# First tile's first 22 rows multiplied beside the product keys, 12 of them summed there

## The chip, the core and the metric

One core of a Trainium2 chip runs the whole program in one launch. The metric is device time in microseconds. The kernel before took 4780.42 us, the median of 3 runs (4776.94 to 4783.93).

## What is computed

The trunk has two layers on 256 context and 512 latent tokens of width 1024: a gated linear attention in layer 0 and a differential attention in layer 1, each followed by a PEER expert mixer (layer 0 on all 6 tiles of 128 tokens, layer 1 on the 4 latent tiles). The change touches the mixer only:

```python
def block(xc):                       # 128 tokens
    q = (xc @ wq).reshape(C, 8, 2, 128)
    s = einsum('chzd,zkd->chzk', q, subkeys)          # 128 keys a side
    top_s, top_i = lax.top_k(s, 16)
    cand_s = top_s[:, :, 0, :, None] + top_s[:, :, 1, None, :]
    best_s, best_j = lax.top_k(cand_s.reshape(...), 16)
    g = softmax(best_s)                               # 8 heads x 16 experts
    ue, ve = u[idx], v[idx]
    act = gelu(einsum('cd,chkd->chk', xc, ue))
    return einsum('chk,chkd->cd', g * act, ve)
```

So every token has 128 pairs (8 heads of 16), each with a row of U and a row of V, out of 16384.

## The kernel before

The stages of a layer follow each other with a meeting of all five engines between them (`run`). Three of them matter here.

**The keys** (`product_keys`) take 16 steps, one for each head and side: step j is side j % 2 of head j // 2. SyncE loads the weights of the step, ScalarE rounds them (L1548), GpSimd subtracts for the low part (L1571), TensorE projects with 24 matmuls for each segment (L1518), ScalarE takes the queries (L1554), TensorE scores them against the keys (L1526), and VectorE finds the strongest 16 of every tile in four rounds (L1590 to L1606). The steps run in a hardware loop, two by two, and projection runs a step ahead of the scores.

**The experts** (`peer`) treat the tiles in two ways. The last ones, three in layer 0 and two in layer 1, are *sparse*: each pair's rows of U and V are gathered from memory. The others are *dense*: all experts are multiplied and a table of gates picks. The choice of a tile (`choose`, L2059 to L2073) searches the best 16 of each head's candidates (`search`), decodes them into key numbers (`decode`) and makes the indices of the gathers and the softmax weights. The order is the first sparse tile, the dense ones, then the other sparse ones. The first sparse tile is decoded in two halves of four heads, so that its gathers can start after the first half.

A sparse row passes through a pipe. GpSimd gathers U into one of 4 slots and V into one of 8 (L1784, L1791), row by row in one order. VectorE multiplies U with the token (`products`, L2081), ScalarE applies gelu (L1899), VectorE multiplies with the weight (`shares`, L2088), and then, for the first tile's first 96 rows, ScalarE makes a diagonal matrix of it (L1913) and TensorE sums the V row with it into PSUM banks 2 and 3 (`spread`, L1801). The later rows are summed by VectorE (L2106). Rows go in groups of two. 6 groups are multiplied beside the second tile's choice, between its pieces; 42 go beside the *lots*.

A lot is 8 tokens of a dense tile: VectorE makes one-hot places (L2112), ScalarE gates them (L1905), TensorE multiplies (L1818), ScalarE takes the result (L1922), and every fourth lot SyncE writes 2 MB of gates to memory. 16 lots are a dense tile: three blocks in layer 0, two in layer 1, and a transposed choice (`turn`, L1808) stands before each block. In layer 0 every lot also has a product of the modulation's weights w_mod (L321) of 0.5 MB, with two buffers: the load (L312) of the next but one waits for the product. At the end of the blocks comes the **key loop** (L1827, L1836), 128 keys of dense scores and values, in which the rest of the rows are gathered and summed.

Of the kernel before, what the change touches and what calls it, by code (L numbers as in the profile page):

```python
# [9 lines left out]
F32 = mybir.dt.float32  # L10
# [41 lines left out]
ROWS_FIRST = (96, 96)  # L52
ROWS_END = KEYS - 2
# [395 lines left out]
def norm(B, layer, gain, shift, scale, segs, split=0, ahead=None):  # L449
# [3 lines left out]
    if split:  # L453
        ar.take(KEYS_AHEAD)
# [1009 lines left out]

def product_keys(B, layer, segs):

    t0, n_tok = segs[0][0], sum(seg[1] for seg in segs)
    tiles = n_tok // P
    top, top_key = best_of(B, tiles)
    top_key = top_key.bitcast(U32)  # L1470
    ar, parts = Arena(B.peer_arena), Arena(B.part_arena)
    w_raw = [ar.take(C * P) for _ in range(2)]
# [5 lines left out]
    found_i = ar.take(tiles * TOPK, U32).rearrange("p (n k) -> p n k", n=tiles)  # L1478
    w_in, w_before = [B.kept(f"keys_w_in{s}") for s in range(2)], 16 * HEADS * layer
    names = ("const_in", "iota_in", "w_high", "w_split", "q_mm", "q_ev", "s_mm", "s_ev", "chain", "passed")  # L1480
    const_in, iota_in, w_high, w_split, q_mm, q_ev, s_mm, s_ev, chain_s, passed = (
        B.kept("keys_const_in") if x == "const_in" else B.sem(x) for x in names)
    ps = B.ps
    ahead_tiles = [tiles - SPARSE_TILES[layer], 0][:SEARCHED[layer]]
    cand = [[ar.take(CAND) for _ in range(2)] for _ in ahead_tiles]
    won, won_j = ([ar.take(TOPK, dt) for _ in ahead_tiles] for dt in (None, U32))
    best, best_j = kept_best(B)
    counted, place = ar.take(P), [ar.take(TOPK, U32) for _ in range(2)]
    PASSES = ((0, 0), (0, 1), (1, 0))
    Q_BANK = (0, 6)  # L1490

    def settle(dve):

        dve.sem_inc(passed, 1)
# [9 lines left out]
    def sync(sp):  # L1504
        sp.dma_start(counted, B.a["iota"]).then_inc(iota_in, 16)
        for j in range(2, 2 * HEADS):
            sp.wait_ge(w_split, j + 1)
            load(sp, j, j % 2)

    def tensor(pe):  # L1510
        def project(j, z):

            pe.wait_ge(w_split, j + 3)
            pe.wait_ge(q_ev, j + 1)
            for (s0, m, which) in segs:
                todo = [(c, a, b) for c in range(C) for a, b in PASSES]
                for at, (c, a, b) in enumerate(todo):
                    mm = pe.matmul(ps[:, Q_BANK[z] + which, 0:m], w[z][:, a, c, :], B.xr[:, b, c, s0:s0 + m],  # L1518
                                   start=at == 0, stop=at == len(todo) - 1)
            mm.then_inc(q_mm, 1)  # L1520

        def score(j, z):
            pe.wait_ge(q_ev, j + 3)
            pe.wait_ge(s_ev, j + 1)
            for t in range(tiles):
                mm = pe.matmul(ps[:, 2 + 2 * z + t // 4, t % 4 * P:t % 4 * P + P],  # L1526
                               q[z][:, t * P:t * P + P], keys[:, z, :], start=True, stop=True)
            mm.then_inc(s_mm, 1)

        pe.sem_inc(q_mm, 2)  # L1530
        pe.wait_ge(const_in, 16 * layer + 16)
        project(0, 0)
        with pe.Fori(0, HEADS - 1) as i:
            project(2 * i + 1, 1)
            score(2 * i, 0)
            project(2 * i + 2, 0)
            score(2 * i + 1, 1)
        project(2 * HEADS - 1, 1)
        score(2 * HEADS - 2, 0)
        score(2 * HEADS - 1, 1)  # L1540

    def scalar(act):
        act.sem_inc(q_ev, 2)

        def split_w(j, z):
            act.wait_ge(w_in[z], 8 * j - 8 * z + 16 + w_before)
            act.wait_ge(q_mm, j + 1)
            act.copy(w[z][:, 0].rearrange("p c n -> p (c n)"), w_raw[z]).then_inc(w_high, 1)  # L1548

        def take(j, z):  # L1550
            act.wait_ge(s_ev, j + 1)
            act.wait_ge(q_mm, j + 3)
            for (s0, m, which) in segs:
                ins = act.copy(q[z][:, s0 - t0:s0 - t0 + m], ps[:, Q_BANK[z] + which, 0:m])  # L1554
            ins.then_inc(q_ev, 1)

        split_w(0, 0)
        split_w(1, 1)
        with act.Fori(0, HEADS - 1) as i:
            for z in range(2):  # L1560
# [696 lines left out]
```

## Time and profile before

| | layer 0 | layer 1 |
|---|---|---|
| keys, TensorE's first projection to VectorE's last | 954 to 1127 | 3434 to 3542 |
| first tile's choice | 1131 to 1159 | 3547 to 3576 |
| second tile's choice with 12 rows | 1159 to 1199 | 3576 to 3616 |
| lots | 1199 to 1566 (48) | 3616 to 3892 (32) |
| key loop | 1590 to 2760 | 3913 to 4730 |

The profiled execution took 4767.23 us, of which 4765.6 are the span from the first to the last instruction; its mean granted TensorE clock is 0.929. Times in the table are us from the span's start. Over the span TensorE is busy 87%, VectorE 70%, GpSimd 38% and ScalarE 27%. A busy share is an average over stages with different limits; the stage tables say which engine is near its bound in each.

### The profile page before, as it was taken

What the parts mean: (1) busy time and instruction counts of PE and PEld (TensorE: products, weight loads), DVE (VectorE), ACT (ScalarE), POOL (GpSimd) and SP (SyncE); (2) the same over time, 40 slices, a digit from 0 to 9 for tenths busy, and PEclk for the clock granted to TensorE, in tenths of its full rate; (3) what the DMA queues carried; (4) which work ended last, traced back from release to release, by engine and by line L of the source; (5) the groups of instructions that cost most, each with busy time, mean ns of one, the idle gap of its engine ahead of it and who ended that gap; (6) DMA issues with size and microseconds to landing.
All of it is one profiled execution on the core that took longest, in us unless ns stands there. A gap on an engine that the chain in (4) does not pass through costs nothing.

```text
span 4765.6 us, 53250 instructions
## 1 busy us (share of the span) xinstructions
PE 4164.2 (87%) x18407; PEld 2864.9 (60%) x18407; DVE 3321.5 (70%) x6651; ACT 1309.2 (27%) x2628; POOL 1799.4 (38%) x1652
## 2 busy tenths in 40 slices
PE   7999976694998899999999979886667879999997
PEld 3776664383776666666666645553353446666665
DVE  2466665568779677787777846676589767777776
ACT  3231311211666211111111123332114552222222
POOL 0012111022665555656566600000127755554452
PEclk8999978797998999999999989997788999999998
DMA  7966785713998999999999936888619999999995
GB/s 242 284 197 199 230 236 145 246 58 116 360 396 330 395 363 400 398 387 390 371 391 391 393 125 175 227 226 224 195 55 331 383 369 399 391 391 400 392 389 226
DMA packets 514577, 1408.03 MB, mean 295 GB/s; under 512 B 45692, under 2 KB 128892, under 8 KB 509470
## 3 DMA queue, kind: packets, MB, share of 16 engines
q1 hardware_dynamic: 330014, 733.73, 46.1%
q0 software_dynamic: 184320, 671.17, 36.4%
q8 instruction: 139, 2.28, 0.2%
q14 instruction: 104, 0.85, 0.1%
HBM read 1226.46 MB, written 178.26 MB: 295 GB/s over the span
## 4 chain that ended last, share of the span: by engine, by line
PE 62%; DVE 14%; DMA 12%; POOL 4%; ACT 4%; issue 3%; SPq 0%; DVEq 0%; ACTq 0%; POOLq 0%
PE ps L1836 19%; PE ps L1827 17%; DMA peer_arena<-in_peer_u 4%; PE ps L1518 3%; DMA u_rows<-mixer_arena 3%; PE ps L746 3%; PE ps L1801 2%; DMA expert_rows<-u_rows,peer_arena 2%; PE ps L1227 2%; PE ps L1232 2%; DVE expert_rows L2081 2%; PE ps L749 2%; PE ps L321 2%; PE ps L815 1%; POOL expert_rows L1791 1%
## 5 line engine op out<-in xcount | busy, mean ns | idle before, releaser
L1784 POOL DMA_INDIRECT expert_rows<-u_rows,peer_arena x640 | 836.8, 1308 | 1038.9 <-DVE expert_rows L2081 809.7
L1827 PE MATMUL ps<-part_arena,peer_part_arena 128*128 128x384 f32 (+1 forms) x4096 | 1028.4, 333 | 39.3 <-DVE peer_part_arena L2118 26.7
L2081 DVE SCALAR_TENSOR_TENSOR expert_rows<-expert_rows,mixer_in 128x1024 f32<-128x1024 f32 x640 | 764.2, 1221 | 140.8 <-DMA expert_rows<-u_rows,peer_arena 138.4
L1791 POOL DMA_INDIRECT expert_rows<-in_peer_v,peer_arena x640 | 760.8, 1189 | 207.0 <-issue 185.2
L1827 PEld LDWEIGHTS ps<-part_arena,peer_part_arena 128*128 128x128 f32 x4096 | 698.5, 189 | 113.9 <-issue 104.3
L1836 PE MATMUL ps<-best,peer_arena 128*128 128x512 f32 x1540 | 685.3, 592 | 0.0
L1827 PE MATMUL ps<-mixer_in_parts,peer_part_arena 128*128 128x384 f32 (+1 forms) x2048 | 633.0, 309 | 0.0
L2106 DVE SCALAR_TENSOR_TENSOR peer_arena<-expert_rows,peer_arena 128x1024 f32<-128x1024 f32 x445 | 571.7, 1285 | 34.7 <-DVE peer_arena L2106 1.4
L1801 PE MATMUL ps<-expert_rows,peer_arena 128*128 128x512 f32 x768 | 376.1, 638 | 163.6 <-ACT peer_arena L1913 163.3
L1836 PEld LDWEIGHTS ps<-best,peer_arena 128*128 128x128 f32 x1540 | 285.1, 189 | 296.0 <-issue 296.0
L1571 POOL TENSOR_TENSOR part_arena<-peer_arena,part_arena 128x1024 fp32r<-128x1024 f32 x32 | 76.5, 2392 | 1004.9 <-ACT part_arena L1548 1004.9
L2118 DVE TENSOR_TENSOR peer_part_arena<-peer_arena,peer_part_arena 128x1024 fp32r<-128x1024 f32 x256 | 312.9, 1222 | 154.0 <-ACT peer_part_arena L1929 153.6
L1827 PEld LDWEIGHTS ps<-mixer_in_parts,peer_part_arena 128*128 128x128 f32 x2048 | 386.6, 189 | 55.0 <-issue 55.0
L1899 ACT ACTIVATE peer_arena<-peer_arena 128x2 f32<-128x2 f32 x320 | 65.3, 204 | 1176.1 <-DVE expert_rows L2081 1176.0
L1801 PEld LDWEIGHTS ps<-expert_rows,peer_arena 128*128 128x128 f32 x768 | 150.7, 206 | 335.9 <-issue 214.4
L1058 POOL TENSOR_TENSOR mixer_arena<-mixer_arena 128x64 f32<-128x64 f32 x168 | 82.4, 490 | 645.1 <-ACT mixer_arena L902 645.1
L2172 DVE TENSOR_TENSOR peer_arena<-peer_arena 128x384 f32<-128x384 f32 (+1 forms) x256 | 124.8, 488 | 254.4 <-ACT peer_arena L1964 254.0
L1929 ACT CAST peer_part_arena<-peer_arena 128x1024 fp32r<-128x1024 f32 x256 | 266.0, 1039 | 110.8 <-DMA peer_arena<-in_peer_u 110.6
L1964 ACT ACTIVATE peer_arena<-ps 128x384 f32<-128x384 f32 (+1 forms) x256 | 110.8, 433 | 558.8 <-PE ps L1827 558.7
L367 DVE STREAM_TRANSPOSE mixer_arena<-mixer_arena 128x512 f32<-128x512 f32 x272 | 169.4, 681 | 117.1 <-DMA u_rows<-mixer_arena 93.9
L1518 PE MATMUL ps<-ffn_in_parts,part_arena 128*128 128x512 f32 (+1 forms) x1152 | 231.6, 360 | 11.7 <-POOL part_arena L1571 11.7
L1836 PE MATMUL ps<-peer_arena 128*128 128x512 f32 x520 | 231.5, 592 | 0.0
(273 smaller groups left out, 6050.9 us busy)
## 6 DMA issues: line engine op xcount, KB each, us to landing
peer_arena<-in_peer_u SPq DMA_DIRECT2D x256, 512.0 KB, 12.8
best<-in_peer_v SPq DMA_DIRECT2D x154, 512.0 KB, 9.0
mixer_arena<-in_peer_u SPq DMA_DIRECT2D x272, 256.0 KB, 7.4
u_rows<-mixer_arena SPq DMA_DIRECT2D x136, 512.0 KB, 4.7
hidden<-in_peer_u SPq DMA_DIRECT2D x240, 256.0 KB, 6.3
u_rows<-hidden SPq DMA_DIRECT2D x120, 512.0 KB, 5.1
gates<-peer_arena SPq DMA_DIRECT2D x20, 2048.0 KB, 10.6
peer_arena<-in_peer_v SPq DMA_DIRECT2D x52, 512.0 KB, 8.1
```

Of the source, the lines that this page charges most:

```text
L367: dve.transpose(self.outside[t][:, b % 2 * 512:b % 2 * 512 + 512], self.inside[s].rearrange("p (a c i) -> p c a i", a=4, i=P)[:, :, :, 32 ...
L746: pe.matmul(out, left, right, start=start, stop=stop)
L1518: mm = pe.matmul(ps[:, Q_BANK[z] + which, 0:m], w[z][:, a, c, :], B.xr[:, b, c, s0:s0 + m], start=at == 0, stop=at == len(todo) - 1)
L1784: pool.indirect_dma_start(u_ring[:, k % U_SLOTS, :], None, u_table, bass.IndirectOffsetOnAxis(u_index[s][:, m:m + 1], 0)).then_inc(u_row_i ...
L1791: pool.indirect_dma_start(v_ring[:, k % V_SLOTS, :], None, v_table, bass.IndirectOffsetOnAxis(v_index[s][:, m:m + 1], 0)).then_inc(v_row_i ...
L1801: mm = pe.matmul(ps[:, 2 + half, :], diag[m % V_SLOTS], v_ring[:, m % V_SLOTS, half * 512:half * 512 + 512], start=m == 0, stop=m == first ...
L1827: mm = pe.matmul(ps[:, 6, 0:dense_tok], left[j % len(left)][:, c, :], right[:, c, :], start=at == 0, stop=at == len(todo) - 1)
L1836: mm = pe.matmul(ps[:, 2 * n + half, :], wt[j % 2][:, n * P:n * P + P], v[j % BUFS][:, half * 512:half * 512 + 512], start=j == 0, stop=j ...
L1929: act.copy(u_high[j % 2], u[j % BUFS]).then_inc(u_rounded, 1)
L2081: dve.scalar_tensor_tensor(out=rows, in0=rows, scalar=1.0, in1=B.x[:, :, rows_at + s * P:rows_at + s * P + P], op0=ALU.mult, op1=ALU.mult, ...
L2106: dve.scalar_tensor_tensor(out=to, in0=rows, scalar=w, in1=to, op0=ALU.mult, op1=ALU.add).then_inc(y_ok, 1)
L2118: dve.tensor_tensor(u_low[j % BUFS], u[j % BUFS], u_high[j % 2].bitcast(F32), ALU.subtract).then_inc(u_split, 1)
```

## The change

Both layers get it. In `product_keys` the hardware loops are unrolled (the find of a step is now `strongest`), and:

- After step 3, when both sides of heads 0 and 1 are known, VectorE chooses these two heads of the first sparse tile (`choose` in the keys: `search_pairs`, `decode_pairs`, `index_pairs`, which are the old `search` and `decode` as functions).
- From step 5 on each step ends with a group of two products: 11 groups, 22 rows. Groups 0 to 7 get their shares two steps later; groups 0 to 5, 12 rows, are summed on TensorE in steps 10 to 15, behind the scores.
- GpSimd gathers U rows 0 to 25 and V rows 0 to 15 there, into 4 + 4 slots of their own, behind the subtraction of each step and after the last step.
- PSUM: banks 2 and 3 are the sum's from the start; of the scores the tiles from the fifth on, and of the queries the context segment, now share one bank for both sides, with a wait for the step before.
- The iota table, which the experts also loaded, is loaded only once, in the keys.

In `peer` the first choice has the other six heads, in one part. 8 groups (11 to 18) are multiplied beside the pieces of both choices; 29 groups in place of 42 are left for the lots. GpSimd goes on with V row 16; U rows follow from 26 on. The loads of w_mod wait for row 15's sum, since their buffers lie on the early slots. The key loop keeps its rows.

```diff
+EARLY_HEADS, CHOSEN_BEHIND, EARLY_FROM = 2, 3, 5
+EARLY_GROUPS, EARLY_GELUS, EARLY_SHARES, EARLY_SUMS = 11, 8, 8, 6
+U_EARLY, V_EARLY = 4, 4
+U_ROWS_EARLY, V_ROWS_EARLY = 26, 16
 # product_keys
     def tensor(pe):
         def project(j):
             z = j % 2
             pe.wait_ge(w_split, j + 1)
             if j >= 2:
                 pe.wait_ge(q_ev, j - 1)
             for (s0, m, which) in segs[::-1]:
                 if which == 0 and j:
                     pe.wait_ge(q_ev, j)
...
+                if t == 4 and j:
+                    pe.wait_ge(s_ev, j)
...
+        for j in range(STEPS):
+            if j + 1 < STEPS:
+                project(j + 1)
+            score(j)
+            if group_at(j) >= 5:            # group_at(j) = j - EARLY_FROM
+                spread(group_at(j) - 5)
     def scalar(act):
...
+        for j in range(STEPS):
+            take(j)
+            if j + 2 < STEPS:
+                split_w(j + 2)
+            if j == CHOSEN_BEHIND + 1:
+                exp()
+            if group_at(j) >= 3:
+                gelus(group_at(j) - 3)
+            if group_at(j) >= 5:
+                diagonals(group_at(j) - 5)
     def gpsimd(pool):
...
+        def gather_u(a):
+            if a == 0:
+                pool.wait_ge(index_ok, 1)
+            for k in range(GROUP * a, GROUP * a + GROUP):
+                if k >= U_EARLY:
+                    pool.wait_ge(score_ok, k - U_EARLY + 1)
...
+        for j in range(STEPS):
+            split_low(j)
+            if group_at(j) >= 1:
+                gather_u(group_at(j) - 1)
+            if group_at(j) >= 6:
+                gather_v(group_at(j) - 6)
+        for a in range(group_at(STEPS) - 1, U_ROWS_EARLY // GROUP):
+            gather_u(a)
+            if a < 13:
+                gather_v(a - 5)
     def vector(dve):
...
+        for j in range(STEPS):
+            strongest(j)
+            if j == CHOSEN_BEHIND:
+                choose()
+            if group_at(j) >= 0:
+                products(group_at(j))
+            if 0 <= group_at(j) - 2 < EARLY_SHARES:
+                shares(group_at(j) - 2)
 # peer
-    AHEAD = 6
+    AHEAD, AHEAD_AT = 8, (0, 3, 5, 8, 10, 13, 15, 18)
+    G0, K0, SUMMED = EARLY_GROUPS, GROUP * EARLY_GROUPS, GROUP * EARLY_SUMS
+    late = slice(EARLY_HEADS, HEADS)
     def gpsimd(pool):
-        for k in range(steps):
+        for k in range(V_ROWS_EARLY, steps):
             s, m = divmod(k, PAIRS)
+            if k == EARLY_HEADS * TOPK:
+                pool.wait_ge(index_ok, 1)
...
+            if k >= U_ROWS_EARLY:
+                if k - U_SLOTS >= K0:
+                    pool.wait_ge(score_ok, k - U_SLOTS + 1 - K0)
+                pool.indirect_dma_start(S.u_row(k), None, u_table, ...)
+            if k - V_SLOTS >= SUMMED:
                 if k - V_SLOTS < first_rows:
+                    pool.wait_ge(s0_mm, k - V_SLOTS + 1 - SUMMED)
...
     def vector(dve):
-        dve.wait_ge(iota_in, 16)
-        for _ in choose(0):
-            pass
         ahead = 0
-        for piece, _ in enumerate(choose(1)):
-            if piece in (0, 2, 4, 6, 8, 9):
-                products(ahead)
+        for piece, _ in enumerate(itertools.chain(choose(0), choose(1))):
+            if piece in AHEAD_AT:
+                products(G0 + ahead)
```

## Rows read from the trace of the kernel before

**Rows 1.** The page: DMA engines, busy tenths in 40 slices

```profile
DMA  7966785713998999999999936888619999999995
```

**Rows 2.** Us; PE, PEld, DVE, ACT, POOL busy; PEclk, DMA share, GB/s (layer 0)

```profile
954.00:1127.10 173.10, 156.82 (x960) 141.33 (x960) 128.62 (x802) 26.98 (x46) 36.05 (x16) 0.95 0.13 43
1130.80:1159.30 28.50, 0.00 (x0) 0.00 (x0) 26.12 (x119) 1.59 (x2) 7.42 (x8) 0.50 0.33 114
1159.30:1199.30 40.00, 22.18 (x46) 9.31 (x46) 35.15 (x115) 7.02 (x19) 27.69 (x24) 0.78 0.89 317
1199.30:1320.90 121.60, 115.76 (x630) 87.25 (x630) 91.67 (x173) 81.40 (x205) 72.28 (x57) 0.92 0.95 365
1320.90:1437.20 116.30, 111.31 (x630) 83.70 (x629) 90.98 (x174) 80.92 (x205) 78.52 (x56) 0.94 1.00 395
1437.20:1565.70 128.50, 108.39 (x584) 78.94 (x584) 114.77 (x275) 79.51 (x200) 70.46 (x52) 0.91 0.90 335
1590.00:2760.00 1170.00, 1165.27 (x4494) 809.96 (x4494) 918.65 (x1257) 204.82 (x394) 692.62 (x568) 1.00 1.01 388
```

**Rows 3.** The same columns, layer 1: keys, two blocks of lots

```profile
3434.00:3542.20 108.20, 95.19 (x484) 80.97 (x482) 87.77 (x544) 21.68 (x29) 33.56 (x14) 0.95 0.19 58
3616.30:3756.00 139.70, 114.95 (x427) 64.85 (x427) 108.36 (x209) 85.93 (x226) 108.11 (x86) 0.91 0.96 361
3756.00:3892.00 136.00, 107.46 (x415) 61.74 (x416) 110.21 (x218) 83.78 (x224) 104.53 (x81) 0.94 0.98 375
```

**Rows 4.** Chain of waits in layer 0's keys: start us, us, what

```profile
982.56 1.34 PE ps L1526 x12
983.89 8.34 PE ps L1518 x48
```

**Rows 5.** VectorE's keys: timeline (layer 0), chain (layer 1)

```profile
993.72 1.29 DVE L1590 MAX8 peer_arena<-ps 128x8 f32<-128x128 f32 x6 [1.21 <-PE ps L1526]
...
3502.13 0.88 DVE peer_arena L1603 x4
3508.72 0.88 DVE peer_arena L1603 x4
3515.02 0.88 DVE peer_arena L1603 x4
```

**Rows 6.** Timeline of VectorE beside the second tile's choice, layer 0

```profile
1160.35 1.22 DVE L2081 SCALAR_TENSOR_TENSOR expert_rows<-expert_rows,mixer_in 128x1024 f32<-128x1024 f32 x1
1161.50 1.22 DVE L2081 SCALAR_TENSOR_TENSOR expert_rows<-expert_rows,mixer_in 128x1024 f32<-128x1024 f32 x1
...
1195.21 0.29 DVE L2072 TENSOR_TENSOR peer_arena<-peer_arena 128x128 f32<-128x128 f32 x1
```

**Rows 7.** 1149 to 1200: a gather, the U gathers' landing, TensorE's first sums

```profile
1163.84 0.94 POOL L1791 DMA_INDIRECT expert_rows<-in_peer_v,peer_arena  x1 [0.30 <-issue]
...
DMA to landing us min/median/max: 4.6/5.8/6.6
...
1168.85 9.25 PE L1801 MATMUL ps<-expert_rows,peer_arena 128*128 128x512 f32 x16 [57.77 <-ACT peer_arena L1913]
```

**Rows 8.** Chain of waits through one lot of layer 0

```profile
1226.94 1.68 PE ps L321 x16
1228.62 1.89 PE ps L1818 x16
1230.51 3.44 PE ps L1801 x8
```

**Rows 9.** Loads of w_mod in layer 0: timeline of SyncE and TensorE, then chain

```profile
1235.66 21.35 SPq L312 DMA_DIRECT2D peer_arena<-in_w_mod  x4
...
1265.38 1.84 PE L321 MATMUL ps<-cond,peer_arena 128*128 128x2 f32 x16
...
1263.69 11.16 DMA peer_arena<-in_w_mod
```

**Rows 10.** The page's group of GpSimd's subtraction in the keys

```profile
L1571 POOL TENSOR_TENSOR part_arena<-peer_arena,part_arena 128x1024 fp32r<-128x1024 f32 x32 | 76.5, 2392 | 1004.9 <-ACT part_arena L1548 1004.9
```

More of the change, by code:

```diff
@@ L1532, in tensor, with spread @@
[L1532 to L1540, printed above, removed]
-    def scalar(act):
-        act.sem_inc(q_ev, 2)
-        def split_w(j, z):
-            act.wait_ge(w_in[z], 8 * j - 8 * z + 16 + w_before)
+        def spread(a):
+            for m in range(GROUP * a, GROUP * a + GROUP):
+                pe.wait_ge(diag_ok, m + 1)
+                pe.wait_ge(v_row_in[m % V_SLOTS], 16 * ((before + m) // V_SLOTS) + 16)
+                for half in range(2):
+                    mm = pe.matmul(ps[:, 2 + half, :], S.diag[m % V_SLOTS], S.v_row(m)[:, half * 512:half * 512 + 512],
+                                   start=m == 0, stop=False)
+                mm.then_inc(s0_mm, 1)
@@ new lines, in products, with shares @@
+        def products(a):
+            for k in range(GROUP * a, GROUP * a + GROUP):
+                dve.wait_ge(u_row_in[k % U_SLOTS], 16 * ((before + k) // U_SLOTS) + 16)
+                rows = S.u_row(k).rearrange("p (c d) -> p c d", c=C)
+                dve.scalar_tensor_tensor(out=rows, in0=rows, scalar=1.0, in1=B.x[:, :, rows_at:rows_at + P],
+                                         op0=ALU.mult, op1=ALU.mult, accum_out=S.score[0][:, k:k + 1]).then_inc(score_ok, 1)
+        def shares(a):
+            cols = slice(GROUP * a, GROUP * a + GROUP)
+            dve.wait_ge(gelu_ok, a + 1)
+            dve.wait_ge(weighed, 1)
+            dve.tensor_tensor(S.share[0][:, cols], S.act_out[0][:, cols], S.weight[0][:, cols], ALU.mult).then_inc(share_ok, 1)
@@ L1851, in tensor @@
             pe.wait_ge(mod.added, 1)
[L1852 removed]
+        for a in range(EARLY_SUMS, G0 + AHEAD - 1):
             spread(a)
@@ new lines, in choose @@
+        def choose(n):
+            heads = slice(0, HEADS) if n else late
+            pairs = slice(heads.start * TOPK, PAIRS)
+            count = heads.stop - heads.start
+            best, best_j = S.kept[n % 2][:, heads], S.kept_j[n % 2][:, heads]
+            yield from search_pairs(dve, chain, settle, top[:, ORDER[n], heads], best, best_j, [x[:, heads] for x in cand])
+            here = gate(n)[:, heads]
+            chain.done(dve, dve.tensor_tensor(here, best, best[:, :, 0:1].to_broadcast([P, count, TOPK]), ALU.subtract))
+            dve.sem_inc(shifted, 1)
+            yield from decode_pairs(dve, chain, S, top_key[:, ORDER[n], heads], S.kept_j[n % 2], pairs, [x[:, heads] for x in differ])
+            if ORDER[n] >= nd:
+                index_pairs(dve, chain, S, layer, ORDER[n] - nd, pairs)
```

519 lines of the change are left out of this document (275 added, 244 removed).

## The prediction

> **What bounds the kernel now.** I read the page's slices first: the DMA engines stand at 8 or 9 nearly wherever an expert stage runs [rows 1]. Then busy time by stage. In layer 0 [rows 2] the keys (954 to 1127) leave the DMA engines at a share of 0.13; the first tile's choice (1130.8 to 1159.3) has VectorE alone, TensorE at zero; the stretch after it (to 1199.3) is VectorE's too, 35.2 of 40.0 us. The three blocks of 16 lots (121.6, 116.3 and 128.5 us) have DMA at 0.90 to 1.00 and TensorE at 108 to 116 busy; the key loop from 1590 to 2760 has both at 1.00. Layer 1 [rows 3] is alike, but its lots (139.7 and 136.0 us) are DMA's alone: share 0.96 and 0.98, VectorE 110 busy, TensorE 107 to 115. So rows gathered during the keys use an idle resource, and a row taken out of the lots is worth what binds there. Against that stands VectorE, which multiplies every row and is the next bound everywhere ahead of the lots.
>
> Who sets the keys differs. In layer 0 a step is 8.34 us of projection and 1.34 us of scores on TensorE, 9.68 us [rows 4]; VectorE idles 1.21 us of it [rows 5], so its own step is 8.47 us. In layer 1 VectorE sets the pace itself: the same instruction comes back after 6.59 and 6.30 us [rows 5], 6.45 on average.
>
> **The change part by part.** First the units. A product takes 1.15 us of VectorE (start to start) [rows 6]; a group of two, with its share of 0.15 us, 2.45 us. A group's sum takes TensorE 3.44 us [rows 8]. A gather costs GpSimd 0.94 us and 0.30 of issue, and lands in 5.8 us while the DMA engines are not full [rows 7]. A row of U and V is 1.05 MB (128 rows of 4 KB, twice).
>
> *Keys, layer 0: +27 us.* VectorE gets the choice of two heads, 22 products and 8 shares. The two heads' choice isn't in the trace. Below it is a quarter of the 28.5 us of a full one [rows 2], 7.1; above it is half, 14.3, since most of its instructions have a fixed cost. I take 10.5: the large ones shrink to a quarter, the small ones don't. So 10.5 + 22 x 1.15 + 8 x 0.15 = 37 us. Step 3, behind which it comes, still starts at 993.7 + 9.7 = 1003.4 [rows 5]. From there VectorE has 13 steps of about 8.55 us (between its 8.47 and what is seen when it waits for nothing) and the 37: 1151.6. TensorE gets 3.44 us in each of steps 10 to 15, a step of 13.1 against VectorE's 11.0, which costs some 3 us more after its lead is used. End near 1154 against 1127. Bounds +24 (no such excess) and +40 (V rows land late and hold the next projection, which is queued behind the sum on TensorE, while GpSimd's wait for a product holds the weights' split queued behind it).
>
> *Keys, layer 1: +36 us.* There is no idle time to use, so all 37 us show, less up to 2.5 us for the loop's turn, which the unrolled steps don't have (every second step is 0.3 longer [rows 5]). TensorE's 6.3 + 3.4 = 9.7 is hidden by a lead of over a step. Bounds +34 and +50.
>
> *Between the stages: +2 us each.* GpSimd's last gathers, U rows 24 and 25 and V rows 14 and 15, can go only after VectorE's last products: 4 gathers of 1.24 us end about 3.9 us later, and the meeting waits for them. The iota load in front of the choice (about 1.9 of the 3.7 us between 1127.1 and 1130.8) falls away. Bounds 0 and +5.
>
> *The choices ahead of the lots: +7 us each.* Before, from 1130.8 to 1199.3, 68.5 us. The second tile's choice ends with the instruction at 1195.21 [rows 6]: 36.2 us, of which 14.2 are 12 products and 5 shares, so 22.0 for itself. Now: six heads 20.1 us (three quarters of the large instructions, most of the small; 28.5 had its decoding twice), 22.0, 8 groups and 3 more shares 19.8, and 1.2 to the turn: 63 us. To that comes a wait which the code makes. GpSimd issues V rows 16 to 25 ahead of U row 26. V rows 20 to 25 wait until rows 12 to 17 are summed, and TensorE starts these after a pause, in which its granted clock is 0.50, 1.2 GHz [rows 2]; before, its first groups took 4.6 us each [rows 7]. V row 25 goes at about +14 us, U row 27 at about +19, and lands at about +25. VectorE wants it in its sixth piece, at +13. What is queued behind it there is the rest of both choices. So some 11 us, and 2 more where rows 32 and 33 wait for the six heads' index: 76 us. Bounds: 63 - 68.5 = -6 (no wait) and +15 (twice the second, a slow landing).
>
> *Lots, layer 0: -33 us.* 84 rows become 58: per block 9.7 groups in place of 14. TensorE falls by 14.9 us to 96 in the second block, VectorE by 10.6 to 104 in the third, bytes from 45.9 MB (395 GB/s x 116.3 us [rows 2]) by 9.1 to 36.8, 94 us. So the blocks go to about 101, 99 and 112 at best, -54. But each load of w_mod can start only after TensorE's product two lots earlier. How long one takes shows only where TensorE waits or nearly does: the load issued at 1263.69 held it for 11.2 us, the one issued at 1256.7 (the last of its four) had landed 8.7 us later [rows 9]. A pair of lots now has 2 x 3.57 + 1.21 x 3.44 = 11.3 us on TensorE [rows 8]; a load of 11.2 us and its product need 11.2 + 1.7 + 0.3 = 13.2. Before, a pair with 13.2 to 14.0 covered that. The DMA engines are less full now, so I take 9.3 us, a wait in about half of the pairs, and 109, 105 and 119: 333 against 366. Bounds -54 and -10.
>
> *Lots, layer 1: -60 us.* No such loads. Bytes per block from 50.7 MB by 13.6 to 37, 97 us at 385 GB/s; VectorE from 109 busy by 15.9 to 93, and some 8 of gaps and the turn, 101; TensorE 85 to 92. Before, the block stood at its DMA bound; now three are close, so I allow 7 over the 101: 108 twice, 216 against 276. Bounds -74 and -36 (120 each).
>
> *The key loop: nothing.* It begins with row 96 as before, on the same rings, with both bounds at 1.00.
>
> *A rule against the change.* In the keys GpSimd's subtraction takes 2.39 us [rows 10], and the instructions of VectorE beside it have one input in SBUF; a product has two. No row shows the pair. The Trainium skill (SBUF — State Buffer, section "SBUF: two separate sides") says that a VectorE instruction with two SBUF inputs and a GpSimd one that reads SBUF take a shared port as an exclusive lock, the later waiting for the whole of the other. By that rule the keys would be longer wherever they meet; it is the second slower rival below.
>
> **The sum.** Layer 0: 27 + 2 + 7 - 33 = +3. Layer 1: 36 + 2 + 7 - 60 = -15. Together -12 us, from 4767.2 us of the profiled execution to 4755. The median of the three runs, 4780.4, is 13.2 above that execution, so 4768 us, 0.25% less.
>
> **The rivals.**
> *The lots fall to their bare bounds* (-54 and -74): -47, 4733; half of the way is 4751. For it: the blocks before stand within 3% of theirs. Against: then one bound was alone.
> *The wait in the choices is not there* (-13 in each layer): 4742. For it: TensorE may sum rows 12 to 17 sooner. Against: U row 26 is behind ten gathers of 1.24 us anyway.
> *Layer 1's lots stop at 120*: +24, 4780, no change. For it: VectorE, ScalarE and TensorE hand each lot on in turn, so three engines near their bounds don't run quite beside each other.
> *Slower, by w_mod.* The load keeps its 11.2 us, as the gathers refill the queue. A pair takes 13.2 us, a block 16 x 6.6 + 9 + 1 = 116, with the cold start 120, 116 and 120: -10 in place of -33, and choices 4 worse: +15, 4795. It decides from a load of 10 us on. For it: the DMA engines stay near 400 GB/s by my own sum. Against: one of the loads shown took under 8.7 us beside just as many gathers.
> *Slower, by products behind the subtraction.* If a step's products wait for it once, 11 x 2.39 = 26 us in each layer, +40, 4820; the sign turns at 0.55 us a step (12 / 22), and 1 us a step, +10, gives 4790. Against: the subtraction follows the end of a projection, which falls in the first half of VectorE's step, and the products are its last 2.3 us.
> That rows don't move at all can't be: the numbers of the groups stand in the code, and only their cost is open.
>
> **How the numbers follow.** Forecast 0.38, bare bounds 0.19, no wait 0.04, layer 1 at 120 us 0.15, w_mod 0.15, subtraction 0.09. About 0.2% is what a measurement can tell here, 9.6 us: faster means under 4771. The forecast's own range, 4755 to 4782, lies across that, 0.24 faster and 0.14 same. Faster is 0.24 + 0.19 + 0.04 = 0.47; same 0.14 + 0.15 = 0.29; slower 0.15 + 0.09 = 0.24. The range 4740 to 4799 leaves out the farther half of the bare bounds and of the subtraction, and takes in w_mod's case. Both signs are in it since it is a difference of two sums, about +81 and -93.
>
> **What would show it.** Keys end near 1154 in layer 0, and last 36 us longer in layer 1, with VectorE without idle time from step 4. The next choice starts 6 us after VectorE's last product. In the choices VectorE has one wait of about 11 us for a U row, at its sixth piece. The first lot comes 76 us after the choice begins. Layer 0's blocks take 109, 105 and 119 us with waits of TensorE for w_mod; layer 1's take 108. The key loops keep their 1170 us and, in layer 1, some 817. Wrong would be: TensorE's granted clock under 0.9 in layer 1's keys, products that wait for rows there, or a key loop that changes.

## The result and the profile after

The changed kernel takes 4790.27 us, the median of 20 runs (4780.06 to 4805.97), against 4781.30 for 20 runs of the kernel before (4764.16 to 4786.75). The medians lie 9.0 us apart and the means 13.0; the ratio over all these runs is 1.0028, 95% interval 1.0019 to 1.0037: slower by 0.28%, some 13 us. The forecast was 4768.0, faster by 0.25%. The time lies inside the stated range of 4740 to 4799, but the sign is wrong.

The profiled execution of the changed kernel took 4802.94 us (span 4801.2, mean granted clock 0.926), at the high end of its runs, while that of before stood at the low end of its own. So I compare stretches, not ends. Here is the view of busy time by stage, with the columns of [rows 2]: layer 0's keys, both choices, the three blocks of lots and the key loop.

```profile
968.20:1174.60 206.40, 184.76 (x1008) 153.22 (x1008) 164.26 (x900) 34.07 (x69) 80.04 (x54) 0.95 0.41 133
1187.80:1263.20 75.40, 51.69 (x108) 21.79 (x108) 59.49 (x208) 13.72 (x40) 45.44 (x42) 0.86 0.81 299
1263.20:1373.30 110.10, 101.19 (x590) 81.93 (x589) 78.71 (x148) 78.53 (x191) 53.73 (x36) 0.88 0.83 311
1373.30:1483.40 110.10, 103.10 (x597) 81.95 (x597) 81.42 (x153) 78.41 (x194) 57.74 (x40) 0.89 0.94 350
1483.40:1600.00 116.60, 93.70 (x539) 75.72 (x539) 105.56 (x257) 77.64 (x190) 51.07 (x37) 0.85 0.77 278
1625.30:2832.70 1207.40, 1202.87 (x4624) 834.03 (x4624) 935.48 (x1279) 208.50 (x400) 697.59 (x568) 1.00 0.98 377
```

Layer 1: keys, choices, two blocks [rows 3].

```profile
3462.40:3617.70 155.30, 131.91 (x560) 100.01 (x560) 127.26 (x644) 29.70 (x53) 79.85 (x54) 0.92 0.54 176
3632.20:3707.00 74.80, 52.26 (x99) 21.66 (x99) 59.62 (x208) 13.58 (x40) 48.53 (x42) 0.81 0.81 290
3707.00:3814.50 107.50, 86.65 (x371) 54.42 (x371) 91.00 (x173) 81.33 (x206) 76.99 (x56) 0.94 0.89 331
3814.50:3922.00 107.50, 80.95 (x350) 49.71 (x351) 93.42 (x184) 76.17 (x199) 78.27 (x56) 0.95 0.92 340
```

The reader is to see three things. Nothing stands between the first two rows but a hole, 1174.6 to 1187.8 (3617.7 to 3632.2 in layer 1), in which little but GpSimd's last four gathers stands. In layer 0's lots the DMA engines' share fell from between 0.90 and 1.00 [rows 2] to between 0.77 and 0.94. And TensorE's granted clock in layer 0's first two blocks went from 0.92 and 0.94 of 2.4 GHz to 0.88 and 0.89.

By the forecast's terms (keys: first projection to the end of VectorE's last instruction; meeting: from there to its first addition in the experts; choices: to the first lot; lots: to the first dense score; key loops: from there to the start of the last dense value, both layers; us):

| | forecast | before | after | difference |
|---|---|---|---|---|
| keys, layer 0 | +27 | 172.8 | 206.4 | +33.6 |
| keys, layer 1 | +36 | 116.7 | 155.3 | +38.6 |
| meeting, layer 0 | +2 | 3.8 | 13.2 | +9.4 |
| meeting, layer 1 | +2 | 5.4 | 14.6 | +9.2 |
| choices, layer 0 | +7 | 69.0 | 75.4 | +6.4 |
| choices, layer 1 | +7 | 69.4 | 74.8 | +5.4 |
| lots, layer 0 | -33 | 389.7 | 362.1 | -27.6 |
| lots, layer 1 | -60 | 296.2 | 238.2 | -58.0 |
| key loops | 0 | 2024.9 | 2027.9 | +3.0 |
| sum | -12 | | | +20.0 |

Of the 35.6 us between the two profiled executions another 14.0 lie before layer 0's keys, where the code is the same; the last runs below bear on these. The lots too scatter by a few us: their mean over all profiled executions with the same code there is 387.4 (8) against 360.5 (6) in layer 0, -26.9, and 300.8 (7) against 237.8 (11) in layer 1, -63.0. With these the sum is +15.7, where the ratio says +13. The key loops' +3.0 is such scatter as well: over all profiled executions their means differ by 1.2 us in layer 0, the other way, and by 0.2 us in layer 1.

The largest miss is the meeting. A *drain* is the instruction behind which an engine reports that its work of the stage is done, and a gather has *landed* when its semaphore tells that its rows are there. The chain of waits in layer 0's meeting (start, us, what); clears of semaphores of some 0.03 us each, with the gaps between them, are left out:

```profile
1173.71 1.68 POOL peer_arena L1753
1175.39 10.20 POOLq L244
1185.60 0.03 SPq L252
...
1187.78 0.39 ACT peer_arena L2105 x3
```

L244 is GpSimd's drain in the meeting, and all five engines wait there for its report. What GpSimd had issued ahead of it, by the timeline:

```profile
1173.71 1.68 POOL L1753 DMA_INDIRECT peer_arena<-u_rows,peer_arena  x1 [5.34 <-DVE peer_arena L1829]
1175.69 0.94 POOL L1753 DMA_INDIRECT peer_arena<-u_rows,peer_arena  x1 [0.30 <-issue]
1176.94 0.94 POOL L1760 DMA_INDIRECT peer_arena<-in_peer_v,peer_arena  x1 [0.30 <-issue]
1178.18 0.94 POOL L1760 DMA_INDIRECT peer_arena<-in_peer_v,peer_arena  x1 [0.30 <-issue]
```

The last issue ends at 1179.12 and its row lands 5.6 us after 1178.18, at 1183.8; the drain ends at 1185.6, and 2.2 us of clearing semaphores and starting follow. The forecast had counted the issues and not the landing.

### The profile page after: what moved, and what is told of

It is laid out like the page before. It is cut to its first block, busy times and chain, and to the rows that moved or that the text cites. A ratio compares the mean times of both kernels' runs of the same rounds, so it can differ in the third digit from the quotient of the medians.

```text
span 4801.2 us, 52809 instructions
## 1 busy us (share of the span) xinstructions
PE 4201.1 (88%) x18407; PEld 2891.9 (60%) x18407; DVE 3323.7 (69%) x6665; ACT 1312.8 (27%) x2634; POOL 1806.6 (38%) x1652
## 4 chain that ended last, share of the span: by engine, by line
PE 62%; DVE 15%; DMA 12%; ACT 3%; POOL 3%; issue 3%; SPq 1%; POOLq 0%; DVEq 0%; ACTq 0%
PE ps L2041 20%; PE ps L2032 17%; DMA peer_arena<-in_peer_u 4%; DMA u_rows<-mixer_arena 3%; PE ps L1660 3%; PE ps L751 2%; PE ps L1232 2%; PE ps L1237 2%; PE ps L2006 2%; PE ps L326 2%; PE ps L754 2%; DMA u_rows<-hidden 2%; DVE expert_rows L2214 2%; PE ps L2023 1%; PE ps L820 1%
## 5 line engine op out<-in xcount | busy, mean ns | idle before, releaser
L1989 POOL DMA_INDIRECT expert_rows<-u_rows,peer_arena x588 | 777.7, 1323 | 1005.6 <-DVE expert_rows L2214 876.5
L1996 POOL DMA_INDIRECT expert_rows<-in_peer_v,peer_arena x608 | 731.3, 1203 | 211.8 <-issue 178.6
L2214 DVE SCALAR_TENSOR_TENSOR expert_rows<-expert_rows,mixer_in 128x1024 f32<-128x1024 f32 x588 | 700.2, 1220 | 94.8 <-DMA expert_rows<-u_rows,peer_arena 92.8
L2006 PE MATMUL ps<-expert_rows,peer_arena 128*128 128x512 f32 x640 | 312.9, 637 | 60.5 <-ACT peer_arena L2120 60.3
L2006 PEld LDWEIGHTS ps<-expert_rows,peer_arena 128*128 128x128 f32 x640 | 126.6, 207 | 206.7 <-issue 133.7
L2023 PE MATMUL ps<-peer_arena 128*128 128x128 f32 x1280 | 190.2, 310 | 62.1 <-ACT peer_arena L2129 39.4
## 6 DMA issues: line engine op xcount, KB each, us to landing
peer_arena<-in_peer_u SPq DMA_DIRECT2D x256, 512.0 KB, 12.6
```

What stands on the lines that cost most here:

```text
L1989: pool.indirect_dma_start(S.u_row(k), None, u_table, bass.IndirectOffsetOnAxis(u_index[s][:, m:m + 1], 0)).then_inc(u_row_in[k % U_SLOTS], 16)
L1996: pool.indirect_dma_start(S.v_row(k), None, v_table, bass.IndirectOffsetOnAxis(v_index[s][:, m:m + 1], 0)).then_inc(v_row_in[k % V_SLOTS], 16)
L2006: mm = pe.matmul(ps[:, 2 + half, :], diag[m % V_SLOTS], S.v_row(m)[:, half * 512:half * 512 + 512], start=False, stop=m == first_rows - 1)
L2023: mm = pe.matmul(ps[:, half, x * P:x * P + P], row[n % 2][:, t, :], col[n % 2][:, t, :], start=True, stop=True)
L2214: dve.scalar_tensor_tensor(out=rows, in0=rows, scalar=1.0, in1=B.x[:, :, rows_at + s * P:rows_at + s * P + P], op0=ALU.mult, op1=ALU.mult, ...
```

## The experiments

**What the drain waits for.** Four kernels, each the kernel before plus DMAs that nobody needs, issued when VectorE has ended the keys. The small gather reads rows of the iota table instead of U:

```diff
+        pool.wait_ge(found_all, 1)          # VectorE, behind its last find
+        for x in range(EXTRA):              # 1, 4, or 1 of 512 bytes a row
+            pool.indirect_dma_start(extra[x][:, 0:EXTRA_WIDTH], None, B.u_rows[layer], ...)
...
         # the fourth kernel, SyncE in place of GpSimd
+        sp.wait_ge(found_all, 1)
...
+        for x in range(EXTRA):              # 4
+            sp.dma_start(B.u_ring[:, x, :], B.u_rows[layer][x * P:x * P + P, :])...
```

> The kernel before, plus one gather of 128 rows of 4 KB that nobody uses: GpSimd issues it when VectorE has ended the keys' last find, just ahead of the meeting of the engines, in each layer. Gap: from the start of VectorE's last find to its first addition in the experts; 4.1 us (layer 0) and 5.6 us (layer 1) in the kernel before, 15.9 and 17.2 in the changed one. Theory 'GpSimd's drain at the meeting ends only when its gathers have landed': start and issue about 2 us, landing about 5.3 us, so +7 to +8 in each layer. Rival 'the drain costs a time of its own for each gather issued, landed or not' (8.65 us over 4 gathers, about 2 each): +4. Rival 'the drain waits for nothing, the changed kernel's gap is semaphores to be cleared and the issue': +1.7 to +2.

> As the run with one gather, but with four, as many as the changed kernel issues behind its last product. Same gap. Drain until landed: 3 more issues of 1.24 us, so 3.7 us over the run with one, +11 to +12 over the kernel before. A price for each gather: +14 to +16. Drain waits for nothing: +5.4.

> As the run with one gather, but of 128 rows of 512 bytes in place of 4 KB. It lands sooner. Drain until landed: the gap is shorter than with the full gather by as much as this one lands sooner (its landing time is in the trace), an estimate of 2 to 3 us. A fixed price of a drain that has a gather before it: the same gap as with the full one, within 0.3 us.

> The kernel before, plus four plain loads of 0.5 MB that SyncE issues when VectorE has ended the keys' last find; GpSimd waits for them in the experts only where its own first wait has it idle for over 20 us. If the drain of every engine waits for the DMAs that it has issued: issue about 1 to 2 us and landing about 6 to 8 us, so +7 to +10 in the gap. If only GpSimd's drain does: +1 to +2, the issues alone.

Chain of waits at the drain (L240 in these kernels) and the issue before it, for one gather, four (chain and last issue), one small:

```profile
1131.80 4.75 POOLq L240
```

```profile
1132.86 10.44 POOLq L240
...
1136.99 0.93 POOL L1578 DMA_INDIRECT peer_arena<-u_rows,peer_arena  x1 [0.30 <-issue]
```

```profile
1135.60 2.99 POOLq L240
```

The single gather was issued at 1132.04 and landed 4.4 us later, at 1136.4; the drain ended at 1136.6. The last of the four landed 6.1 us after 1136.99, at 1143.1; the drain ended at 1143.3. The small one, issued at 1135.84, landed 2.6 us later, at 1138.4; the drain ended at 1138.6. Three times the drain ends within 0.2 us of the last landing, and in layer 1 it does so three times more: neither a fixed price nor one for each gather gives 2.99, 4.75 and 10.44. The gap grew by 4.6 and 4.5 us with one gather (expected 7 to 8: the issue took 1.1 us and the landing 4.4 from the issue's start, not 2 and 5.3), by 10.3 and 9.8 with four (11 to 12). The 4.6 alone would also fit a price for each gather (+4), but that gives 14 to 16 for four. In the small one's run it grew by 4.2 and 2.6, but 1.4 of layer 0's is the iota load behind it, which took 3.1 us instead of 1.7. In the changed kernel the drain ends 1.8 us behind the last landing, in both layers; that rest is open.

The fourth kernel's gap grew by 4.9 and 4.0 us, between both expectations, for a reason that neither names. The chain:

```profile
1132.50 0.43 SPq L1515
...
1132.98 0.13 SPq L240
...
1134.85 4.77 DMA peer_arena<-in_iota
```

SyncE's drain took 0.13 us with four loads in flight. It doesn't wait for landings; the iota load that follows queued behind the four (4.8 us, not 1.7).

**The same in the changed kernel, and the order of the gathers.** n1 leaves GpSimd's drains out between the keys and the experts (every row is awaited by its own semaphore anyway). n2 adds an order in which U rows 26 to 29 go sooner. u1 has the order alone.

```diff
-                engine.drain().then_inc(stage_done, 1)
+                if which == "gpsimd" and stage.get("go_on"):      # the keys
+                    engine.sem_inc(stage_done, 1)
+                else:
+                    engine.drain().then_inc(stage_done, 1)
...
-                    engine.drain()
+                    if which != "gpsimd" or not stage.get("no_drain"):   # the experts
+                        engine.drain()
...
         # n2 and u1
+        U_BEHIND = {18: (26, 27), 22: (28, 29), 27: (30,), 28: (31,)}
+        for k in range(V_ROWS_EARLY, steps):
...
+            if k >= 32:
+                gather_u(k)
+            gather_v(k)
+            for x in U_BEHIND.get(k, ()):
+                gather_u(x)
```

> The changed kernel, but GpSimd goes from the keys to the experts without its two drains (it only reports itself at the meeting). Theory 'the drain waits until the gathers have landed and all engines wait for it': the time from VectorE's last product to its first addition falls from 13.2 and 14.5 us to about 6.5 to 8, as GpSimd reports itself when its last issue ends, 4.6 us after the last product; together -12 to -14 us, from a ratio of 1.0028 against the kernel before to about 0.9999. Rival 'the time goes into clearing semaphores': below 1 us for each layer, ratio 1.0025 or so. Rival 'the gain is eaten, since the experts' first rows have not landed then': the gap falls but the first lot comes as late as in the changed kernel.

> The run without GpSimd's drains, and U rows 26 to 29 are gathered between V rows 18 and 23, not behind V row 25. Theory 'VectorE's wait of 9.8 us in the choices is the order in which GpSimd issues': the wait falls to under 2 us, the first lot comes 8 to 10 us sooner in each layer, -16 to -20 us over the run before it, ratio about 0.996. Rival 'V rows then come later and TensorE's sums end the choices, or the lots start with fewer rows ahead': under half of that, ratio 0.998 or above.

> The changed kernel with U rows 26 to 29 gathered between V rows 18 and 23, and GpSimd's drains as they were. If the two edits are independent, VectorE's wait of 9.8 us in the choices falls to under 2.5, the gap at the meeting stays at 15.9 and 17.2, and the ratio is 1.0028 less 16 us, 0.9995; with 0.9986 for the drains alone and 0.9959 for both, 1.0000.

Ratios to the kernel before: n1 0.9986 (0.9974 to 0.9998), n2 0.9959 (0.9942 to 0.9975), u1 0.9987 (0.9977 to 0.9997). n1 came out better than the 0.9999 expected. In it the time from VectorE's last product to its first addition is 2.3 and 3.4 us, less than the 6.5 to 8 expected:

```profile
1164.47 1.22 DVE L1834 SCALAR_TENSOR_TENSOR peer_arena<-peer_arena,mixer_in 128x1024 f32<-128x1024 f32 x1
...
1166.81 0.94 POOL L1758 DMA_INDIRECT peer_arena<-u_rows,peer_arena  x1 [0.30 <-issue]
1167.96 0.80 DVE L1512 TENSOR_TENSOR spare_arena<-best 128x96 f32<-128x96 f32 x3 [2.26 <-SPq L256]
1168.06 0.97 POOL L1765 DMA_INDIRECT peer_arena<-in_peer_v,peer_arena  x1 [0.30 <-SPq L256]
```

The experts' first addition starts while GpSimd still has its V gathers of the keys to issue: a plain increment doesn't even wait for the gathers ahead of it. Part of the gain is eaten, as one rival said: the wait in the choices grows from 9.8 to 12.6 us in layer 0, and the choices take 77.9 and 75.8 us.

The waits of VectorE in layer 0's choices (us in total, times, longest), in the changed kernel and in n2:

```profile
DVE expert_rows L2214 <- DMA expert_rows<-u_rows,peer_arena: 12.0, 3, 9.8
```

```profile
DVE expert_rows L2229 <- DMA expert_rows<-u_rows,peer_arena: 5.6, 5, 1.4
```

With the order of n2 the choices take 68.9 and 67.7 us, 9.0 and 8.1 less than in n1, as they took 69.0 and 69.4 before the change. u1 has 66.7 and 66.8 us there with gaps as in the changed kernel; 0.9987 is better than the 0.9995 to 1.0000 expected, by about what the interval allows.

**One layer.** o1 has the change in layer 1 alone, o1n2 the same with both edits of n2.

```diff
-            keys = make(product_keys, layer, segs)
+            keys = make(product_keys if layer == 1 else product_keys_plain, layer, segs)
...
-                       keys, make(peer, layer, segs)]
+                       keys, make(peer if layer == 1 else peer_plain, layer, segs)]
```

> The change in layer 1 alone; layer 0's keys and experts are those of the kernel before, all drains as they were. From the stretches of the two profiled executions: layer 1 alone gives keys +38.5, meeting +9.3, choice +5.4, lots -58, key loop +3, together about -2 to -5 us, layer 0 +22. So this kernel should be at a ratio of 0.999 to 1.0 against the kernel before. If layer 0 is not what makes the change slower, it stays at 1.002 to 1.003.

> The change in layer 1 alone, with both edits of the run with U rows first (no drains of GpSimd between keys and experts, U rows 26 to 29 sooner) in that layer. Expected: layer 1's -2 to -5, -6 for the meeting and -8 to -10 for the wait: -17 to -20 us, ratio about 0.996. If layer 0 gains by the edits as much as layer 1 does, it loses 22 - 16 = 6 us there and the run with both layers is the slower one of the two by that.

The ratios are 0.9984 (0.9972 to 0.9995) for o1 and 0.9943 (0.9928 to 0.9959) for o1n2. Layer 1 alone gains, as its lines of the table say; layer 0 is where the change loses. o1n2 came out better than the 0.996 expected: against the mean of the profiled executions with layer 1 as before, its keys up to VectorE's last find are 38 us longer, the gap from there to the first addition 0.5, the choices 1.3 shorter, the lots 61 and the key loop 2, which is -26 us or 0.9945. The -58 in the table is on the small side, and the key loops' +3 isn't the change's.

**What holds layer 0's lots.** wa and wb leave out all but two loads of w_mod in the experts of layer 0, in the changed kernel and in the one before; their products run on old data, so layer 1's modulation isn't computed from w_mod in them. b3, on n2, keeps the loads and gives w_mod a third buffer.

```diff
         # wa, wb
-                    mod.load(sp, m, m % 2)
+                    sp.wait_ge(mod.used, m + 1)
+                    sp.sem_inc(mod.w_in[m % 2], 16)
...
         # b3
-    mod = ModTiles(B, (ar, Arena(y_tok[1])), "mod", ...)
+    mod = ThreeTiles(B, (ar, Arena(y_tok[1]), Arena(y_tok[0])), "mod", ...)
...
-                    mod.load(sp, m, m % 2)
+                    mod.load(sp, m, m % 3)
```

> The changed kernel; in layer 0's experts only the first two loads of w_mod are made, the other 46 are left out (the products run on what lies in the two buffers, so layer 1's modulation is not the reference's). The lots of layer 0 took 362.1 us from the first to the first dense score. Theory 'they fell by 28 us in place of 33 since TensorE waits 8.8 us for w_mod, and is granted 0.88 in place of 0.93 as it idles more': without the waits at least -9, and with the clock back at 0.93 some 5 us more for each block, to 340 to 350. Rival 'the hand-over of each lot between ScalarE, VectorE and TensorE sets the blocks': over 358.

> The kernel before with the same loads left out. Its lots of layer 0 took 389.7 us with the DMA engines at 0.90 to 1.00. If the DMA engines set these blocks, 8 MB less in each of 46 take them down by more than the changed kernel's, to TensorE's busy time: 3 x 111 + 26, about 360. If TensorE sets them, within 5 us of 389.7.

> The run with U rows first and without GpSimd's drains, and w_mod gets a third buffer in layer 0's experts, so that a load waits for the product three lots back, not two; the bytes are the same. That run's lots of layer 0 took 362.0 us; without the loads it was 334.3. Theory 'latency: TensorE waits 8.8 us for w_mod and then gets a lower clock': the waits fall to about 2, the granted clock in the blocks rises from 0.88 or 0.89 towards 0.92, the lots take 345 to 352, ratio about 0.993 to 0.994. Rival 'traffic: the loads' 25 MB share the DMA engines with the gathers': the lots stay within 4 us of 362, ratio 0.996.

The lots take 334.3 us in wa, 28 less than in the changed kernel and below the 340 expected; in wb 381.7, 8 less than before, where full DMA engines would have given 360. So in the kernel before it was not the DMA engines, in spite of their share of 0.90 to 1.00, that set most of these blocks; TensorE was busy 112 of 116 us in wb's first. And without the loads the change is worth 47 us in these lots. b3 says that what the loads cost in the changed kernel is their latency and not their bytes: 338.1 us (expected 345 to 352) against n2's 362.0, a ratio of 0.9910 (0.9890 to 0.9931). In the changed kernel TensorE's waits for w_mod (three blocks, us, times, longest) are only

```profile
PE ps L326 <- DMA peer_arena<-in_w_mod: 8.8, 5, 3.3
```

and there is none in b3. n2 had 9.0 us of them. The other 15 of the 24 us go with the granted clock of the first two blocks of b3 (same columns), against 0.88 and 0.89 above:

```profile
1237.40:1333.30 95.90, 90.95 (x590) 73.22 (x589) 78.86 (x148) 78.52 (x191) 57.93 (x36) 0.96 0.89 342
1333.30:1435.00 101.70, 96.60 (x597) 76.52 (x597) 81.11 (x154) 78.21 (x194) 59.30 (x40) 0.95 0.98 373
1435.00:1551.00 116.00, 93.50 (x541) 75.42 (x541) 105.18 (x254) 77.21 (x190) 51.12 (x37) 0.85 0.80 291
```

**The keys.** k2, on n2, lets GpSimd issue the V rows of a step ahead of its U rows. b3k2 has this order and b3's third buffer.

```diff
         for j in range(STEPS):
             split_low(j)
+            if group_at(j) >= 6:
+                gather_v(group_at(j) - 6)
             if group_at(j) >= 1:
                 gather_u(group_at(j) - 1)
-            if group_at(j) >= 6:
-                gather_v(group_at(j) - 6)
```

> The run with U rows first in the experts and without drains, and in the keys' steps 11 to 15 GpSimd issues its two V rows ahead of the two U rows, so that V rows no longer stand behind a wait for VectorE's product. Layer 0's keys took 203.7 us to VectorE's last find, with a step of 14.0 us in which TensorE waited 2.4 us for a V row and summed the first group in 6.7 us. Theory 'part of the excess over the forecast is the V row': that step falls to 11 to 12 us, the keys of layer 0 to 200 or 201, ratio 0.0005 to 0.001 lower than 0.9959. Rival 'U rows come 2.5 us later then and VectorE waits for them, or the split behind them is late': keys as long or longer in one of the two layers.

> Both edits together on the run with U rows first and without drains. If both theories hold they touch different stages and add: ratio about 0.992 to 0.993. If neither does: 0.996.

TensorE's timeline around its first early sum, changed kernel and k2:

```profile
1094.07 0.71 PE L1672 MATMUL ps<-peer_arena 128*128 128x128 f32 x4 [0.79 <-DVEq L1796]
1097.18 6.71 PE L1681 MATMUL ps<-peer_arena 128*128 128x512 f32 x8 [2.40 <-DMA peer_arena<-in_peer_v,peer_arena]
1103.33 8.90 PE L1660 MATMUL ps<-ffn_in_parts,part_arena 128*128 128x512 f32 x48
```

```profile
1083.94 0.71 PE L1677 MATMUL ps<-peer_arena 128*128 128x128 f32 x4 [0.77 <-DVEq L1801]
1084.49 3.60 PE L1686 MATMUL ps<-peer_arena 128*128 128x512 f32 x8
1087.53 8.92 PE L1665 MATMUL ps<-ffn_in_parts,part_arena 128*128 128x512 f32 x48
```

The wait of 2.40 us is gone and the group takes 3.60 us in place of 6.71. VectorE's steps there, measured from its last find to the next, are 11.1 and 10.8 us in place of 14.0 and 12.8. The keys fall by 6.3 us against n2 in layer 0 (expected 3 to 4) and by 8.4 in layer 1, where one step had been 11.7 to 12.2 us and is now 8.3. Not all of layer 0's 6.3 is the edit's: in n1, whose keys are those of the changed kernel, the first step took 11.1 us too and the keys 202.6, only 2 more than in k2, while the six other executions with these keys took 204 to 207. In layer 1 k2 and b3k2 are below all others, 148 and 149 against 155 to 158. TensorE's waits for V rows in layer 1's keys went from 8.0 to 3.8 us, those for GpSimd's split stayed at 11. The ratio is 0.9924 for k2 (0.9901 to 0.9947; 0.9949 to 0.9954 expected) and 0.9891 for both edits (0.9871 to 0.9911; 0.992 to 0.993 expected). b3k2, at 4723.46 us against 4779.75 in its own comparison, beats both kernels: 1.1% less than the kernel before.

**The 14 us before the keys.** The two kernels once more, for a second profile each.

> The changed kernel once more, for a second profiled execution. What lies before layer 0's keys (954.2 us in the kernel before, 968.2 in the changed one, same code but for where the first weights are put) should spread by as much as the runs of one kernel do: if the 14 us belong to the change, the keys start at 965 or later again; if not, they can start anywhere from 955 to 968. The meetings should again take 13 to 15 us from VectorE's last product to its first addition.

> The kernel before once more, for a second profiled execution. Its layer 0 keys started at 954.2 us; the kernels with the change in layer 0 start them at 963 to 971, the others at 954 to 966. If the start belongs to the kernel's code, it is again near 954; if it is chance, it may be anywhere up to 966.

Layer 0's keys began at 968.7 us in the changed kernel's second execution and at 960.0 in that of before; but in b3, k2 and b3k2, which have the change in layer 0 and ran on the chip of that 960.0, at 957.6, 958.2 and 955.3. On another chip it is the other way: n1 and n2 began at 963.1 and 963.5, o1 and o1n2, without the change in layer 0, at 955.0 and 959.1; on a third the changed kernel's second execution, wa and u1 began at 964.0 to 971.3 and wb at 965.7. On the three chips the means differ by -3, +6 and +2 us, and one kernel's start by up to 6, so no run shows that the 14 us are the change's; a few us of them could be. The gap from last find to first addition was 16.0 and 16.8 us again.

## Why the forecast was wrong

**Between the stages, +2 each: this step failed.** 9.4 and 9.2 us were measured, 14.6 over the forecast for both. The step said that the last four gathers "end about 3.9 us later, and the meeting waits for them", and took the end of the issue for the end. The bounds, 0 and +5, left out the row that stood beside it: a gather lands in 5.8 us [rows 7]. And the trace of the kernel before had the answer, at a meeting where it costs nothing, since the other engines end later. At the end of layer 0's experts GpSimd's drain has gathers ahead of it (the drain, the last issue, that gather's landing):

```profile
L239 POOLq DRAIN  x1: 13107/13107/13107, 2755.1 to 2755.1; - x1
2758.96 0.94 POOL L1791 DMA_INDIRECT expert_rows<-in_peer_v,peer_arena  x1 [0.30 <-issue]
DMA to landing us min/median/max: 5.9/5.9/5.9
```

The drain ends at 2768.2, 8.3 us after the last issue has ended and 3.4 after its row has landed. With 3.9 + 5.8 us, less the iota load's 1.9, the step would have been +8. Taking that value would have turned the sum of -12 into 0.

**Keys, layer 0, +27: under-sized, +33.6.** The step had the right mechanism: steps under TensorE's sums take 12.8 to 13.1 us, as forecast 13.1. But the excess of these steps over VectorE's pace of 10.7 is 10.3 us, not 3, as TensorE had less of a lead than I gave it, and some 3 of it is the first V row, which came late in this execution. That was in the bounds (+40); in k2, and in n1 too, the step takes 11.1 us and not 14.0.

**Keys, layer 1, +36: right in sum (+38.6), by other parts.** The choice of two heads took 9.9 us, not 10.5, and a step with two products 8.3. But the words that TensorE's 9.7 us a step "is hidden by a lead of over a step" were wrong: five steps take 9.4 to 11.7 us, and 9.8 is TensorE's own pace. TensorE waited 8.0 us for V rows, which k2 shows to be dear. It also waited 11.1 us for GpSimd's split, 7.9 of it at once, while GpSimd stood 12.9 us for the index of the two heads; but VectorE was busy with that choice then, and k2 is faster with the same 11 us.

**Choices, +7 each: right.** 75.4 and 74.8 us against 76; one wait of 9.8 us for a U row at the sixth piece, where 11 were forecast. n2 and u1 show that the order of issue was its cause: the choices take 66.7 to 68.9 us there.

**Lots, layer 0, -33: right mechanism, over-sized by 5.** The blocks took 110, 110 and 117 us against 109, 105 and 119. TensorE waited for w_mod five times, 8.8 us in all, less than "in about half of the pairs". What the step lacked is the clock: it took a matmul's time from a TensorE that was busy 111 to 116 of 116 to 122 us at 0.92 to 0.94. With gaps the clock was 0.88, and in these two blocks the sums' matmuls went from 0.61 to 0.62 us each on the mean, the lots' from 0.31 to 0.32. The Trainium skill (TensorE: Matmul & The Clock Gate, section "HAM oscillation — how this bites in real kernels") says that gaps in TensorE's work bring its clock down; the first two rows of b3 agree, as the clock came back to 0.96 and 0.95 when the waits went.

**Lots, layer 1, -60: right**, 107.5 us twice against 108. **Key loops: right.**

**The rivals.** "Bare bounds" and "the wait is not there" didn't happen: layer 0's lots gave 28 us of 54, and the wait was there. "Layer 1's lots stop at 120" was added up wrongly: -36 in place of -60 makes the sum +12 and the time 4792, slower, not 4780 and "no change", so its chance of 0.15 belonged to slower (0.39 in place of 0.24). That time lies near the measured one, but by luck, as these lots took 107.5 us twice. Two small sums in the choices are 0.3 us off as well (12 products and 5 shares are 14.55 us, 8 groups and 3 shares 20.05), without effect on the 63. "Slower, by w_mod" was not the cause of the sign, though b3 shows that its place was the dearest one left. "Products behind the subtraction" didn't happen: all products in the keys took 1.22 us. But the lock that it rests on can be seen in another instruction. The subtraction of layer 1 that starts at 3564.85 and ends at 3567.27, and VectorE's copy of the found values, which takes 0.20 us elsewhere:

```profile
3564.85 2.42 POOL L1744 TENSOR_TENSOR part_arena<-peer_arena,part_arena 128x1024 fp32r<-128x1024 f32 x1
```

```profile
3565.88 1.44 DVE L1804 TENSOR_SCALAR best<-peer_arena 128x64 f32<-128x64 f32 x1
```

It ends at 3567.32, with the subtraction. This happened 4 times in 32 steps (1.26, 1.40, 1.44 and 0.34 us), 3.6 us in all; the 145 maxima and replacements that ran beside a subtraction took their usual time, at most 0.30 us. The kernel before had it in its trace too, where the place numbers are made ahead of the first scores: four VectorE instructions of only 16 elements a partition (L1579) took 1.9 to 2.3 us beside subtractions. The Trainium skill (SBUF — State Buffer, section "SBUF: two separate sides") says that a VectorE operation in a two-port mode and a GpSimd one hold the pair exclusively, the later waiting for the whole of the other; the trace agrees for this one. No product ran beside a subtraction, so its case of two SBUF inputs stays untested here.

With the meeting as measured the forecast's sum is +3, with the keys as measured too it is +12, against +13 by the ratio. That the time lay inside the range is no merit of the mechanism: the meeting's +9.4 and +9.2 lay outside their bounds of 0 and +5.
